# Attention scores written head by head, and the merge's sums issued ahead of the last weighted sum

## What is computed

```python
def dilated_attn_prompt(q, k, v, window, dil):
    # query t reads keys t - dil*j, j = 0..window//dil
    ...
    sc = jnp.einsum('brnqhd,brnkhd->brnhqk', qb, kk).astype(jnp.float32) * (HEAD_DIM ** -0.5)
    ...
    sc = jnp.where(mask[:, None], sc, NEG_INF)
    lse = jax.nn.logsumexp(sc, axis=-1)
    p = jnp.exp(sc - lse[..., None])
    o = jnp.einsum('brnhqk,brnkhd->brnqhd', p.astype(v.dtype), vv)

# even_mixer: three groups (window, dilation) = (128,1), (512,4), (2048,16), four head slots each
alpha = jax.nn.softmax(jnp.stack(lses, axis=0), axis=0)
y_b = jnp.sum(jnp.stack(outs, axis=0).astype(jnp.float32) * alpha[..., None], axis=0)
y = jnp.concatenate([y_a, y_b], axis=-1) @ w_out
```

## Time and profile before

| | us |
|---|---|
| median of 3 runs | 1164.78 |
| lowest and highest | 1162.54, 1170.73 |
| profiled execution | 1161.33 |
| its span, first to last instruction | 1159.6 |
| PE busy in the span | 1030.2 (89%) |
| DVE busy | 427.2 (37%) |
| ACT busy | 209.5 (18%) |

### The profile page before, as it was taken

One profiled execution on the slowest core, in us unless ns is written; L12 is line 12 of the kernel. 1 busy time (PEld: TensorE's weight loads), 2 busy tenths in 40 slices (PEclk: granted clock), 3 DMA queues, 4 the chain that ended last, 5 costly groups with the idle time before them and its releaser, 6 DMA issues.

```text
span 1159.6 us, 19198 instructions
## 1 busy us (share of the span) xinstructions
PE 1030.2 (89%) x7043; PEld 654.5 (56%) x7044; DVE 427.2 (37%) x906; ACT 209.5 (18%) x425; POOL 182.5 (16%) x270
## 2 busy tenths in 40 slices
PE   6999998879899987788389989988998999999980
PEld 4887786545655544344167767744566555555540
DVE  3441002454722111111149899635363121111216
ACT  4000102232201110110140101144120111111113
POOL 1000010000042221211103120110004222323120
PEclk9999999989899998898899999999988999999995
DMA  9424023345479999999752010164047999999956
GB/s 359 207 103 160 16 111 75 144 183 219 149 257 409 408 409 409 408 409 412 312 224 73 26 48 1 34 248 186 37 179 230 407 406 402 410 407 397 400 206 233
DMA packets 74512, 281.61 MB, mean 243 GB/s; under 512 B 13182, under 2 KB 13886, under 8 KB 71296
## 3 DMA queue, kind: packets, MB, share of 16 engines
q1 hardware_dynamic: 58192, 253.76, 56.1%
q0 software_dynamic: 11120, 17.89, 4.4%
q10 hardware_dynamic: 5120, 8.87, 2.3%
HBM read 270.75 MB, written 29.65 MB: 259 GB/s over the span
## 4 chain that ended last, share of the span: by engine, by line
PE 63%; DMA 21%; DVE 11%; ACT 2%; issue 2%; SPq 0%; POOLq 0%; DVEq 0%; ACTq 0%; POOL 0%
DMA ring<-w_moe 12%; PE psum L2177 12%; PE psum L2081 7%; DMA ar<-w_moe 6%; PE psum L2244 6%; PE psum L1852 6%; PE psum L2284 5%; PE psum L1808 5%; DVE ar L1711 5%; PE psum L2309 3%; PE psum L1921 2%; PE psum L2160 2%; DVE X L1426 2%; PE psum L2209 1%; PE psum L1796 1%
## 5 line engine op out<-in xcount | busy, mean ns | idle before, releaser
L2177 PE MATMUL psum<-ring,ar 128*64 128x256 f32 x1408 | 175.1, 393 | 18.7 <-DMA ring<-w_moe 16.7
L2177 PEld LDWEIGHTS psum<-ring,ar 128*64 128x64 f32 x1408 | 100.2, 141 | 89.8 <-issue 26.0
L2284 PE MATMUL psum<-ar,ring 128*128 128x272 f32 x512 | 121.3, 398 | 5.3 <-DVE ar L1697 2.9
L2284 PEld LDWEIGHTS psum<-ar,ring 128*128 128x128 f32 x512 | 97.7, 192 | 30.1 <-issue 4.2
L1711 DVE SCALAR_TENSOR_TENSOR ar<-ar,sv 128x512 f32<-128x512 f32 x120 | 107.0, 893 | 5.8 <-ACT ar L1049 1.9
L1634 DVE COPY ar<-psum 128x128 f32<-128x128 f32 x64 | 18.6, 291 | 241.8 <-PE psum L2234 238.3
L2081 PE MATMUL psum<-ring,ar 128*128 128x512 f32 x192 | 90.0, 618 | 4.4 <-DVE ar L1411 4.4
L2177 PE MATMUL psum<-ar 128*64 128x256 f32 x640 | 82.9, 404 | 7.9 <-DMA ar<-w_moe 7.9
L2244 PE MATMUL psum<-ring,ar 128*64 128x512 f32 x352 | 84.1, 599 | 0.8 <-DVE ar L1634 0.8
L2177 PEld LDWEIGHTS psum<-ar 128*64 128x64 f32 x640 | 46.3, 145 | 43.0 <-issue 12.4
L973 ACT ACTIVATE ar<-psum 128x128 f32<-128x128 f32 x64 | 17.7, 277 | 285.9 <-PE psum L2177 285.9
(11 more groups left out here) (266 smaller groups left out, 1211.8 us busy)
## 6 DMA issues: line engine op xcount, KB each, us to landing
ring<-w_moe SPq DMA_DIRECT2D x44, 2048.0 KB, 16.6
ring<-w_moe SPq DMA_DIRECT2D x44, 1024.0 KB, 18.6
ar<-w_moe SPq DMA_DIRECT2D x20, 2048.0 KB, 16.4
ar<-w_moe SPq DMA_DIRECT2D x20, 1024.0 KB, 18.4
ring<-w_pw SPq DMA_DIRECT2D x6, 2048.0 KB, 10.8
ring<-w_mix SPq DMA_DIRECT2D x3, 3072.0 KB, 29.9
ring<-expert_outputs SPq DMA_DIRECT2D x6, 1024.0 KB, 9.1
ring<-kv_in SPq DMA_DIRECT2D x2, 2880.0 KB, 11.1
```

The lines of the kernel that those rows point to most:

```text
L2177: t = mm(psum[64 * f:64 * f + 64, u % 2, 0:2 * P], xt[:, k, 64 * (u % 2):64 * (u % 2) + 64], w[:, k, f, :], start=k == 0, stop=k == KD - 1)
L2284: t = mm(psum[:, glu_bank(m) + h, 0:HALF], w[:, k, o:o + P], hT2[:, k, HALF * h:HALF * h + HALF], start=k == 0, stop=k == KD - 1)
```

## The change

It has three parts. In `scores(n)` the loop over the two heads becomes the outer one: all masks and scores of head 0, then all of head 1. Each head's part waits for its own exponentials of the pair before (`exp_done` 4 * n - 2 for head 0, 4 * n for head 1), and `s_done` rises for each head at the end of its part. The four permutation matmuls of the merge move ahead of `weighted(7)`. On ACT the small exponential of the merge moves ahead of the second big copy.

```diff
@@ ACT @@
             for c in range(2):
+                if c:
+                    act.wait_ge(max_ready, 17)
+                    nc.scalar.activation(shares[:, 0:32], shares[:, 0:32], ACT.Exp).then_inc(exp_done, 1)
                 act.wait_ge(o_done, 4 * c + 4)
                 act.wait_ge(pt_done, 2 * c + 14)
                 nc.scalar.activation(view(A_SC + 1024 * c, 1024, "p (k q) -> p k q", k=2),
                                      psum[:, 4 + 2 * c:6 + 2 * c, :], ACT.Copy).then_inc(o_copied, 1)
-            act.wait_ge(max_ready, 17)
-            nc.scalar.activation(shares[:, 0:32], shares[:, 0:32], ACT.Exp).then_inc(exp_done, 1)
-
@@ PE, scores(n) @@
-                else:
-                    pe.wait_ge(exp_done, 4 * n)
-                for t_, lo, hi in spans(n):
-                    o = (P if kind == 0 else 3 * P) + 2 * P - (hi - lo)
-                    for hh in range(2):
+                for hh in range(2):
+                    rows_ = slice(64 * hh, 64 * hh + 64)
+                    if n:
+                        pe.wait_ge(exp_done, 4 * n - 2 + 2 * hh)
+                    for t_, lo, hi in spans(n):
+                        o = (P if kind == 0 else 3 * P) + 2 * P - (hi - lo)
                         mm(psum[:, hh, lo:hi], mb[:, 0:P], mb[:, o:o + hi - lo], start=True, stop=False)
-                    for g in range(1 + kind):
-                        m = 2 * (g + kind) + c
-                        q = slice(t_, SEQ, 4) if kind else slice(P * t_, P * t_ + P)
-                        keys = slice(t_, SEQ, 4) if kind else slice(P * t_ + P - (hi - lo), P * t_ + P)
-                        for hh in range(2):
-                            rows_ = slice(64 * hh, 64 * hh + 64)
+                        for g in range(1 + kind):
+                            m = 2 * (g + kind) + c
+                            q = slice(t_, SEQ, 4) if kind else slice(P * t_, P * t_ + P)
+                            keys = slice(t_, SEQ, 4) if kind else slice(P * t_ + P - (hi - lo), P * t_ + P)
                             out = psum[:, hh, lo + P * g:lo + P * g + P] if kind else psum[:, hh, lo:hi]
                             t = mm(out, qkT[rows_, m, q], qkT[rows_, 6 + m, keys], start=False, stop=g == kind,
                                    tile_position=(64 * hh, 0))
-                            if g == kind and t_ % 2:
-                                t.then_inc(s_done, 1)
+                    t.then_inc(s_done, 1)
@@ PE, end of the attention @@
-            weighted(7)
 
             last = stt.rearrange("p s k t h -> p s k (t h)")[:, :, 1, :]
             pe.wait_ge(exp_done, 32)
...
             t.then_inc(stats_moved, 1)
+            weighted(7)
+
```

## The result

The changed kernel takes 1190.23 us (median of 6 runs, 1186.17 to 1192.10) beside 1168.63 us for the kernel before in the same runs: ratio 1.0198, interval 1.0179 to 1.0218, so 2% or some 23 us slower. I had said 1171 us, +7, with 1162 to 1179 as the range. The sign was right, the size was not.

What follows compares the result with a forecast made beforehand. PE's attention work was taken to move everything behind it: 15.9 us more work, 5.5 returned (+10.35), merge -2.1, so +8.2; clock -1.2 gives +7.0. From a median of 1164.8 that made 1171 us, range 1162 to 1179.

Steps and rivals of the forecast that it cites:

- What bounds the kernel; from stage to end: Attention stage ahead of the out projection: whatever PE gains or loses by 260.15 us is gained or lost at the end.
- The work that the reordering adds to PE: Scores of the eight pairs: heads no longer run side by side, 15.9 us more PE work; 1.44 or 0.84 a head and span.
- The bound from below: Strided pairs: a lone record still takes its full step of about 0.23 us, since a lone strided load is as slow.
- rival (b): Strided pairs: a lone record takes half a step, so the kernel is not slower, 1163 us; chance 0.13.
- Rival (c): One head's scores: each load waits for the matmul before on the same rows, strided steps about 0.44 us, 1188 us; chance 0.05.
- The finer waits: Ahead of scores(1), (2), (5), (6): waiting head by head can return at most 6.8 us; 5.5 of the 15.9 come back.
- The merge: End of the stage: moved sums fill PE's idle time and DVE starts the merge 2.26 us sooner; saving 2.1 us.
- The clock: Attention stage: fewer waits may remove stretches at 1.2 GHz, half an array at work may do the contrary; taken as -1.2 us.
- the sum at equal clock: Whole stage without any clock effect: +10.35 us from the scores less 2.1 from the merge, +8.2 us.
- rival (d): Attention stage: half an array at work gets 1.2 GHz for more of it, up to +20 over +8, 1190 at most; chance 0.08.

Runs made afterwards that it cites:

- e3: Kernel before, but inside each span head 0's mask and scores, then head 1's, with the old wait and no merge part; ratio 1.0204 to before.
- e2: Kernel before with only the head-by-head scores and their finer waits, without the merge part; ratio 1.0200 to before.
- e1: Kernel before with only the merge part, the two moves on PE and ACT; 1164.05 us against 1167.23, ratio 0.9967.
- e9: The changed kernel run once more, unaltered, for a second profile; ratio 1.0140 to before.
- e7: Changed kernel with each score matmul taking all 128 rows instead of one head's 64, so its attention is not the reference's; ratio 0.9944 to before.
- e4: Kernel before with each pair's masks and scores written twice, both times with the two heads in turn; ratio 1.0161 to before.
- e5: Changed kernel with one 512-column mask matmul a head ahead of both spans, replacing two of 256, in six of eight pairs; ratio 1.0134 to before.
- e6: Kernel before with the merge part and one 512-column mask matmul a head for both spans of a pair; 1159.94 us against 1166.15, ratio 0.9950.
- e8: Changed kernel with, from pair 1 on, the other head's matmul issued unread beside each score matmul on the other half; ratio 1.0112 to before.

## Why the prediction was wrong, step by step

**What bounds the kernel; from stage to end.** Right: +22.6 us in the stage, +23.75 at the end of layer 0.

**The work that the reordering adds to PE.** Right in each pitch: 0.84 and 1.44 us a head and span at full clock, in the first profile after. The bound from below also held: a lone strided record takes the full step, so rival (b) is out. The step is the same 1.30 us a group at either clock (the L1972 rows at 202.60 and 217.98), so it does not hang on PE's clock.

**Rival (c),** each load waiting for the matmul before on the same rows, is out: four records of one head take 1.30 us, with steps of 0.23 us and not 0.44 behind the first one. The first step, behind the mask, is 0.42 us, as it is in before. The rule of the Trainium skill (TensorE: Matmul & The Clock Gate, Part 3, The mechanism), that a load overlaps a running matmul only where the row group differs, is not borne out here.

**The finer waits.** PE's waits for exponentials fell from 6.8 us to 1.2 us, as counted (0.45 and 0.71 us left, ahead of scores(1) and scores(2)). Only 3 us of it are the finer wait's (profiles of e3 and e2); the rest any longer PE work would have swallowed.

**The merge.** Right: 2.1 us expected, 2.6 us in the profile of e1, 3.9 us with 1.3 to 6.5 by time.

**The clock: the step that failed.** "Fewer waits may remove such stretches [...] but half an array at work may do the contrary. I take -1.2." It was about +15. The line between the profiles of e2 and the changed kernel gives 0.35 us of stage for each us at the lower clock, and 92.15 - 0.35 x (59 - 17) = 77.5 us is what the stage would have been at the clock of before, beside the 69.57 + 8.2 = 77.8 of my sum. That line hangs on two profiles, and e9 lay 1.2 us off it, so it is good to some 3 us. A count of PE's work gives the same without it: 10.3 us for the transposes, weighted sums and sample products, which are the same work in both; 4.1 for the seven contiguous heads and spans at the lower clock, the first in part (1.48 for 0.84); 1.3 for the eleven strided ones (1.56 for 1.44); less the 0.7 that the scores of before lose to it: 15.0 us. So the sum at equal clock holds about as well as this can be told, and nearly the whole miss is this one term: rival (d), to which I gave 0.08. Its price of up to 20 us was of the right size, but its end of 1190 us was counted from the profiled 1161.3; from the median of 1164.8 it would have been 1193. I had set it low because in before the clock was full from 206.6 to 233.6 us and had fallen behind a wait, and took PE's busy time for what keeps the clock up. But in before the scores had never run with half of the array empty, so its rows could not speak for that case, and I should have kept both ends.

**Shown and not shown.** Shown: the clock of before returns with both halves or all rows at work, at the same order (e7), at as many layout changes and as long a stage (e4); it does not return with the old wait (e3) nor with fewer layout changes (e5). Not separated: whether it is the empty half as such that counts, or that PE gets less matmul work done in the same time, which goes with it (484 records in 92 us in the changed kernel, 612 in 90 us in e4); no run has half of the array at work with as many records. Argued only: that the stretches at 0.50 over transposes (the whole array) and weighted sums (two heads on the two halves of its columns) are an aftereffect of the scores ahead of them. Open: why the profile of e2 has 34 us at the lower clock and both of the changed kernel have 59, with the same scores.

## What to carry to other kernels

Where two small matmuls can stand on two halves of the array, issue them next to each other: taking them apart loses the overlap, adds changes of layout at which the next weights are loaded late (0.3 us each here), and can cost the clock of everything around, and the last was the largest of the three. A busy PE is no promise of a full clock; before splitting array-filling work in time, read how the clock stood where the array was half empty, and if no row shows it, keep the price of the lower clock over the whole stage in the range. A change of two parts is worth taking apart: one half of this one was good, and with the masks joined it gives 0.995.

## What the runs showed of the hardware

- With the scores on one half of the array at a time the stage gets 1.2 GHz more often, though PE is busy for 86 to 91% of it: 34 to 60 us of 82 to 93 at the lower level (e2, e3, e5, e9, the changed kernel), against 9 to 18 of 65 to 90 with both halves or all rows filled (before, e1, e4, e6, e7). Adding 44 matmuls that nobody reads made the kernel 10 us faster (e8; weaker against e9).
- Going from whole-array to half-array matmuls and back costs 0.3 us at full clock, strided or not (e7 against the changed kernel).
- Operands with stride 4 in f32 make PE take 0.23 us a record of 128 columns behind the first one, at either clock, alone or with a neighbour; a whole-array load takes 308 ns in place of 190. The Trainium skill tells of 16-byte lines in SBUF (SBUF — State Buffer, Door 1: The DMA port swizzle, the note on SBUF "cachelines"), of which such an access hits a new one with each element; the rows agree with that, and no run here varied the stride.
